# The last down group of a two-layer decoder trunk, multiplied in float32 instead of in three float16 passes

## The reference

```python
def conv_ffn(h, w_up, conv_w, conv_b, w_down):       # w_up 1024 x 5632, w_down 2816 x 1024
    u = causal_dwconv(h @ w_up, conv_w) + conv_b
    gate, up = jnp.split(u, 2, axis=-1)
    return (jax.nn.silu(gate) * up) @ w_down

for layer in range(2):
    x = x + mixer[layer](rmsnorm(x, g))              # layer 0: conv + sparse attention, layer 1: SGU + gated linear attention
    x = x + conv_ffn(rmsnorm(x, ffn_norm[layer]), ...)
```

## Time and profile before

| | |
|---|---|
| median of 3 runs | 2206.64 us (2205.05 to 2211.54) |
| the profiled execution | 2201.6 us, span 2199.9 us |
| PE busy | 2070.1 us, 94% of the span |
| DVE busy | 1398.4 us, 64% |
| POOL busy | 1104.3 us, 50% |
| ACT busy | 1100.4 us, 50% |
| weight loads (PEld) busy | 1006.8 us, 46% |

### The profile page before, as it was taken

One profiled execution on the slowest core, in us unless ns is written; L12 is line 12 of the kernel. 1 busy time (PEld: TensorE's weight loads), 2 busy tenths in 40 slices (PEclk: granted clock), 3 DMA queues, 4 the chain that ended last, 5 costly groups with the idle time before them and its releaser, 6 DMA issues. The chain is left out here.

```text
span 2199.9 us, 30123 instructions
## 1 busy us (share of the span) xinstructions
PE 2070.1 (94%) x11334; PEld 1006.8 (46%) x11334; DVE 1398.4 (64%) x2239; ACT 1100.4 (50%) x1649; POOL 1104.3 (50%) x842
## 2 busy tenths in 40 slices
PE   7989967789999999999999999989999999999998
PEld 3544425554444444444444444556444444444444
DVE  9788888857665575575544036595857467467552
ACT  6459856644664564555323215243566456454520
POOL 6103423315676766757584023403476766765742
PEclk8999988999999999999999999899999999999999
DMA  4002110002111211112232001101211211211112
GB/s 173 20 4 55 31 30 1 13 13 70 48 52 56 66 58 57 55 53 62 68 107 58 0 20 39 49 1 37 70 39 48 68 57 52 71 57 53 58 37 98
DMA packets 186496, 110.22 MB, mean 50 GB/s; under 512 B 4352, under 2 KB 180903, under 8 KB 186359
## 3 DMA queue, kind: packets, MB, share of 16 engines
q1 hardware_dynamic: 185894, 107.00, 16.3%
q0 software_dynamic: 464, 1.39, 0.2%
HBM read 104.18 MB, written 4.19 MB: 49 GB/s over the span
## 5 line engine op out<-in xcount | busy, mean ns | idle before, releaser
L1215 PE MATMUL ps<-arena 128*128 128x512 f16 x2712 | 593.8, 379 | 5.2 <-DVE ps L2745 5.2
L1215 PEld LDWEIGHTS ps<-arena 128*128 128x128 f16 x2712 | 264.7, 98 | 327.1 <-DVE ps L2745 8.2
L1215 PE MATMUL ps<-h_hi,arena 128*128 128x512 f16 x1216 | 369.5, 379 | 15.2 <-DVE arena L2836 6.2
L767 POOL TENSOR_SCALAR w_scaled<-stage 128x1024 f32<-128x1024 f32 (+4 forms) x82 | 80.1, 977 | 586.0 <-PE ps L1075 405.5
L2754 DVE SCALAR_TENSOR_TENSOR work<-ps,fvec,work 128x1023 f32<-128x1023 f32 (+1 forms) x176 | 221.5, 1279 | 18.3 <-ACT work L1949 15.1
L1215 PE MATMUL ps<-h_lo,arena 128*128 128x512 f16 x608 | 230.4, 379 | 0.0
L1215 PEld LDWEIGHTS ps<-h_hi,arena 128*128 128x128 f16 x1216 | 119.0, 98 | 160.8 <-issue 11.4
L1075 PE MATMUL ps<-arena 128*128 128x512 f16 x708 | 159.1, 387 | 13.0 <-DVE xT L2633 5.9
L821 POOL TENSOR_TENSOR w_scaled<-stage 128x512 f32<-128x512 f32 (+2 forms) x62 | 70.0, 1129 | 191.9 <-ACT stage L1681 191.3
L1681 ACT ACTIVATE stage<-stage 128x2048 f32<-128x2048 f32 (+2 forms) x62 | 104.6, 1686 | 107.7 <-DMA stage<-in_ffn_w_up_dram 91.6
L1075 PE MATMUL ps<-h_hi,arena 128*128 128x512 f16 x576 | 148.9, 379 | 3.1 <-ACT small L1853 1.7
(11 more groups left out here) (368 smaller groups left out, 3874.4 us busy)
## 6 DMA issues: line engine op xcount, KB each, us to landing
stage<-in_ffn_w_up_dram SPq DMA_DIRECT2D x84, 512.0 KB, 3.8
stage<-in_ffn_w_down_dram SPq DMA_DIRECT2D x48, 384.0 KB, 3.2
stage<-in_od_w_in_dram SPq DMA_DIRECT2D x20, 512.0 KB, 3.8
stage<-in_ev_w_in_dram SPq DMA_DIRECT2D x12, 512.0 KB, 3.7
arena<-in_x_dram SPq DMA_DIRECT2D x8, 512.0 KB, 6.4
stage<-in_ffn_w_down_dram SPq DMA_DIRECT2D x16, 256.0 KB, 2.7
out_dram<-arena SPq DMA_DIRECT2D x8, 512.0 KB, 3.5
stage<-in_od_w_out_dram SPq DMA_DIRECT2D x12, 256.0 KB, 2.7
```

What stands on the lines that cost most here:

```text
L767: nc.gpsimd.tensor_scalar(scaled, src, W_SCALE, 1.0, ALU.mult, ALU.mult).then_inc(w_parts, 1)
L1215: last = mm(ps[:, bank, :], left, b[:, k, :], start=(fresh and k == 0 and pss == 0), stop=(k == nk - 1 and pss == 2), skip_group_check=True)
```

## The change

For layer 1 only, the last group's gated tiles stay float32: of each tile ACT copies tokens 0 to 511 out of PSUM and DVE tokens 512 to 1023, into the memory where the two float16 rows stood. POOL makes one scaled float32 copy of the weights (`w_whole`) in place of the three instructions of `split`. TensorE runs `down_whole`: the units, the interleaving of the first two and the loop are as before, with one float32 matmul of 128 x 512 in place of three float16 ones. In the tail, turns 4 to 7 no longer stand inside unit 7 but behind the last matmul, with turns 8 to 15. DVE's written order of adds and turns at the end is the same, and so are the waits of SP's loads and stores.

```diff
--- before.py
+++ after.py
@@ -219,6 +219,8 @@
 
         hid_hi = Rows([view(4608 + 512 * k, [T], F16) for k in range(6)])
         hid_lo = Rows([view(7680 if k == 0 else 1536 + 512 * k, [T], F16) for k in range(6)])
+        hid_half = [[view(4608 + 512 * k, [HALF]), view(7680 if k == 0 else 1536 + 512 * k, [HALF])] for k in range(6)]
+        w_whole = [view(-A_FRONT + 1024 * u, [6 * P]) for u in range(2)]
         plain_h = view(0, [2 * KT, HALF])
         top_hi, top_lo = view(8192, [3, 4, HALF], F16), view(8192 + 3072, [3, 4, HALF], F16)
         set_hi, set_lo = ([{nk: view(14336 + 3584 * s + 1792 * part, [7, nk * P], F16) for nk in (2, 3, 4)} for s in range(2)]
@@ -920,7 +922,10 @@
                     split_woven(nf * P)
                     return
                 for m in range(KT):
-                    split_ring(unit0["down1c"] + m, m, nf * P, ring0["down1c"] + m)
+                    n, s = unit0["down1c"] + m, m % 2
+                    pool.wait_ge(w_landed[s], n * 8 + (16 - 8 * s))
+                    pool.wait_ge(unit_done, ring0["down1c"] + m - 1)
+                    G.tensor_scalar(w_whole[s], stage[:, s, 0:nf * P], W_SCALE, 1.0, ALU.mult, ALU.mult).then_inc(w_split, 1)
 
             for i, k in enumerate(TW_BY_POOL):
                 pool.wait_ge(x_landed[k], 32)
@@ -1150,10 +1155,52 @@
                 plain(FIRST)
                 plain(SECOND)
 
+                def whole(m, p0, k, hf, nf):
+                    return mm(pair(p0 + m)[:, hf * HALF:(hf + 1) * HALF], w_whole[m][:, k * P:(k + 1) * P], hid_half[k][hf],
+                              start=(k == 0), stop=(k == nf - 1))
+
+                def down_whole(f0, nf, at):
+
+                    p0, ready = 2 * bank_set(f0 + nf - 2), unit0["down1c"] + 1
+                    pe.wait_ge(x_added, at + 2)
+                    pe.wait_ge(hid_f, FT + f0 + nf - 1)
+                    for m, k0, k1 in ((0, 0, nf - 1), (1, 0, nf - 2), (0, nf - 1, nf), (1, nf - 2, nf)):
+                        if k0 == 0:
+                            pe.wait_ge(w_split, ready + m)
+                        for k in range(k0, k1):
+                            if m == 0 and k in (0, nf - 2, nf - 1):
+                                pe.wait_ge(hid_done, 2 + FT + f0 + {0: nf - 2, nf - 2: nf - 1, nf - 1: nf}[k])
+                            for hf in range(2):
+                                last = whole(m, p0, k, hf, nf)
+                        if k1 == nf:
+                            last.then_inc(unit_done, 1)
+                    with pe.Fori(0, 2) as i:
+                        for mi in range(2):
+                            pe.wait_ge(x_added, i * 2 + (at + 3 + mi))
+                            pe.wait_ge(w_split, i * 2 + (ready + 2 + mi))
+                            for k in range(nf):
+                                for hf in range(2):
+                                    last = whole(mi, p0, k, hf, nf)
+                            last.then_inc(unit_done, 1)
+                    for hf in range(2):
+                        for mi in range(2):
+                            if hf == 0:
+                                pe.wait_ge(x_added, 2 + at + 5 + mi)
+                                pe.wait_ge(w_split, ready + 6 + mi)
+                            for k in range(nf):
+                                last = whole(mi, p0, k, hf, nf)
+                                if (hf, mi, k) == (1, 0, 2):
+                                    turns_out(0, 4)
+                            last.then_inc(unit_done, 1)
+                    turns_out(4, 16)
+
                 def down():
 
                     f0, nf = GROUPS[-1]
                     at = DOWN_AT[layer, len(GROUPS) - 1]
+                    if layer == 1:
+                        down_whole(f0, nf, at)
+                        return
                     name, p0, early = f"down{layer}c", 2 * bank_set(f0 + nf - 2), 10 - nf
 
                     def part(m, k0, k1):
@@ -1168,14 +1215,12 @@
...
-                    else:
-                        tail_units(at, nf, [[w[:, mi, :] for mi in range(2)] for w in (w_hi, w_lo)], hid_hi, hid_lo, 0,
-                                   (p0, p0 + 1), [ready + 6 + mi for mi in range(2)],
-                                   {(1, 0, 2): lambda: turns_out(0, 4), (1, 1, 1): lambda: turns_out(4, 8)})
-                        turns_out(8, 16)
...
@@ -1963,7 +2002,9 @@
                 def highs(f):
                     x, z, y, v = (4 * bank_set(f) + b for b in range(4))
                     act.wait_ge(hid_f, c0 + f + 1)
-                    if not blocked(f):
+                    if layer == 1 and not blocked(f):
+                        A(hid_half[f - LAST][0], ps[:, 4 * bank_set(f) + 2, :], ACT.Copy).then_inc(hid_hi_done, 1)
+                    elif not blocked(f):
                         A(hid_hi.rows[f - LAST], pair(2 * bank_set(f) + 1), ACT.Copy).then_inc(hid_hi_done, 1)
                     elif f % 2 == 0:
                         keep(0, 0, ps[:, y, :])
@@ -2793,7 +2834,10 @@
                 def chain_end(f):
                     at = 4 * bank_set(f)
                     x, z, y, v = (ps[:, at + b, :] for b in range(4))
-                    if not blocked(f):
+                    if layer == 1 and not blocked(f):
+                        dve.wait_ge(hid_hi_done, hid_high_at[layer, f, "all"])
+                        V.tensor_copy(hid_half[f - LAST][1], ps[:, 4 * bank_set(f) + 3, :]).then_inc(hid_done, 1)
+                    elif not blocked(f):
                         dve.wait_ge(hid_hi_done, hid_high_at[layer, f, "all"])
                         V.tensor_tensor(hid_lo.rows[f - LAST], pair(2 * bank_set(f) + 1), hid_hi.rows[f - LAST],
                                         ALU.subtract).then_inc(hid_done, 1)
```

More of the change, by code:

```diff
@@ L1169, in part @@
                             last.then_inc(unit_done, 1)
-                    ready, step = unit0[name] + 1, 1
-                    if layer == 0:
-                        ready, step = unit0["down0c_and_tm"], 2
+                    ready, step = unit0["down0c_and_tm"], 2
                     pe.wait_ge(x_added, at + 2)
                     pe.wait_ge(hid_f, FT * layer + f0 + nf - 1)
-                    pe.wait_ge(w_split, unit0["down0c_and_tm"] + 1 if step == 2 else ready)
+                    pe.wait_ge(w_split, unit0["down0c_and_tm"] + 1)
                     part(0, 0, nf - 1)
-                    pe.wait_ge(w_split, unit0["down0c_and_tm"] + 2 if step == 2 else ready + 1)
+                    pe.wait_ge(w_split, unit0["down0c_and_tm"] + 2)
                     part(1, 0, early)
@@ L1186, in down @@
                             three_pass(mi, nf, hid_hi, hid_lo, 0, pair(p0 + mi), True, True).then_inc(unit_done, 1)
[L1187 to L1190, removed]
-                    else:
-                        tail_units(at, nf, [[w[:, mi, :] for mi in range(2)] for w in (w_hi, w_lo)], hid_hi, hid_lo, 0,
-                                   (p0, p0 + 1), [ready + 6 + mi for mi in range(2)],
-                                   {(1, 0, 2): lambda: turns_out(0, 4), (1, 1, 1): lambda: turns_out(4, 8)})
-                        turns_out(8, 16)
+                    tail_units(at, nf, (tail_hi, tail_lo), hid_hi, hid_lo, 0, (p0, p0 + 1),
+                               [woven("down", 6 + mi) + 1 for mi in range(2)],
+                               {(1, 0, 3): lambda: norm_sums(2, 0), (1, 1, 1): lambda: spread(2, 0)})
                 def item(p):
```

## The result

The changed kernel takes 2225.02 us (median of 4 runs, 2221.52 to 2228.14) against 2206.4 before: ratio 1.0082, 95% interval 1.0064 to 1.0099. It is slower by 18.6 us, where 19.2 were forecast, and the time forecast was 2225.8, from the median of 2206.64 that was known then.

A forecast was written before the change was run, and what follows sets the result against it. TensorE streaming was taken to bound the last group: 63.65 + 7.01 = 70.66 us before, 82.8 + 7.01 + 0.1 = 89.9 after, so 2206.64 + 19.2 = 2225.8 us; range 2217 to 2234.

The forecast's parts named there:

- The price of a float32 matmul: TensorE, last down group: 96 float32 matmuls make 192 records of 0.43 us, 82.6 us; 0.47 us a record as upper end.
- Half price: Rival: a full-size float32 matmul needs only 0.43 us in all, giving 2184.5 us, faster; chance 0.05.
- Weight loads covered: TensorE's float32 weight loads of 0.192 us overlap neighbouring records, priced at nothing; uncovered they would add 37 us.
- The stall at unit 2: TensorE's 1.10 us wait for POOL's split of unit 2's weights goes, covered by 3.4 us of unit 1's matmuls.
- Gated tiles: ACT's copy falls from 1.02 to about 0.60 us, DVE's from 1.22 to 0.69; worth nothing, at most 1.0 us gained.
- The tail: Behind the last matmul: DVE's last add just in time for turn 12; 0.1 us, up to 0.7; stores up to 1.
- Two signs that failed: Expected in the profile: group's first matmul at 2123 us as before, last matmul some 21 us later with 12 turns behind.
- The sum: TensorE's group and turns: 70.66 us before, 89.9 after, a difference of +19.2 us.

The follow-up runs named there:

- f16_unit2_apart: Kernel before, with unit 2's split weights in buffers of their own so POOL can split them earlier; 2202.37 against 2205.77 us, ratio 0.9991.
- turns_as_matmul: Kernel before, with the 64 output transposes done as ordinary float32 matmuls against the identity; 2211.32 against 2205.93 us, ratio 1.0025.
- the float16 kernel's two profiles: Kernel before, with turns 4 to 7 moved behind the last matmul, profiled twice; 2208.73 against 2205.93 us, ratio 1.0009.

## Why the prediction was right

- **The price of a float32 matmul.** Taken as two records of 0.43 us, from a row of 512 columns and 16 partitions; it is two of 0.429, with 128 partitions as well. The whole forecast stood on this term, and choosing the row that agreed in columns was the right choice between the two. Had the row with 128 partitions been scaled up to 0.47 us, the group would have come out 7.8 us too dear.
- **Half price.** Fell twice: by 192 records for 96 calls in the changed kernel, and by the transposes turned into products.
- **Weight loads covered.** Right at 512 columns and, in the experiment, at 256.
- **The stall at unit 2.** Gone, as forecast. I took it at its idle time of 1.1 us; by starts, and by f16_unit2_apart, it is 1.3.
- **Gated tiles.** Nothing, as forecast, and with a named cover: the last tile was copied at 2140.1, 9.6 us behind the group's start, and TensorE needed it at 15.5. The experiment with half the k tiles took that cover away and the wait appeared. What I had not priced is what such a wait can do to the clock; here there was none to pay for.
- **The tail.** 0.1 us taken, nothing measured. The term priced a later start of the last eviction, and that isn't what the end hangs on: in turns_as_matmul the last store was issued 1.2 us closer to the end at no cost. Turn 12, and with it the last add, is what counts. That danger I had named, and it is covered by 0.4 us. The stores, which I had down for up to 1 us, cost 1.9 and 1.7 in the float16 kernel's two profiles and nothing in float32: the price came with a trickle of DMA work that the float32 kernel does not have there. That it was free here I had not worked out; whether an instruction-queue transfer meets the stores was in no row of mine.
- **Two signs that failed.** The group's first matmul was to come at 2123 us again and came at 2130.5. Unchanged code moves by more than that from profile to profile (2123.1 to 2131.9), so the sign could not tell anything; the distance from the group's start could. The last matmul was to end some 21 us later. That was a slip in adding: four turns more stand behind it, so it is 19.2 less 1.75, 17.4 us, and measured from the group's start it is 84.3 against 67.1, 17.2.
- **The sum.** 19.2 forecast; 18.9 in the profile from the group's start, 18.6 and 18.8 in the medians. The 0.3 left are the tail's 0.1 and 0.2 for entering and leaving float32, of which nothing is to be seen: 192 x 0.4292 is the whole 82.4.

## What to carry to other kernels

Three float16 passes cost three quarters of one float32 matmul at 512 columns (0.65 against 0.86 us), so by these prices float32 pays only where making the split operands, and not TensorE, is what the path waits for. Price an operation that a kernel is to get from the nearest row of its own trace with the same free size, and count its records against the calls. And when work is taken off a bound engine, ask which later producer it now overtakes: such a stall may cost more than its idle time. The last instruction of the chain is not always what sets the end: look whether the stores behind it wait for something earlier.

## What the hardware showed beside this

- A float32 product is two records whose spacing is 0.4292 us at 512 columns, 0.2158 at 256, and 0.112 to 0.1175 at 128; a float32 transpose of 128 columns is one record of 0.110.
- TensorE's clock behind idle time: after 4.33 us of it the granted clock was 0.53 over the next 5.1 us, after 2.67 us it was 0.61 over 4.4, and after stalls of 0.6 to 1.2 us in the group it stayed at 1.00. Behind the stall of 2.9 to 3.1 us ahead of the group it fell in nine profiles, after 2.90 us in one of them, and stayed at 1.00 in three, after 3.01 us in one. So at these lengths the length alone doesn't decide; what does these runs don't say.
- Stores of 512 KB that follow one another moved at some 410 GB/s. The trickle behind them, at a sixteenth of that, stood in just the three of twelve profiles in which an instruction-queue transfer started among the stores. It cost nothing in a pause and 1.7 to 1.9 us at the end of the last stores.
- In ten of the twelve profiles the end came 6.8 us behind the issue of the first of the last four stores; the other two, with the trickle last, took 8.5 and 8.7 us. The issue of the last one varied by 1.2 us at no cost.
